# A tile of zeros set by VectorE for TensorE's dummy work at the start of a decoder layer, 17 matmuls in place of 13 transposes

## The chip, the cores and the metric

The kernel runs on one core of one Trainium2 chip. The metric is the time on the device in microseconds (us), the median of several runs. TensorE has two clock levels in what follows, 1.2 and 2.4 GHz.

## The reference

The reference is one hybrid decoder layer over 512 tokens and 1024 channels, all in float32. What is computed first matters here: a projection of the tokens with `w_in`.

```python
proj = h @ w_in[l]                      # (512 x 1024) @ (1024 x 4376)
q, k_c, v_c, k_s, v_s, k_w, v_w, nsa_gl, u, v, merge_gl = jnp.split(proj, splits, axis=-1)
...
o_nsa = native_sparse_attention(q, ...)            # 8 heads, 3 branches
o_sgu = spatial_gating(u, v, ...)
merged = g_nsa * (o_nsa @ w_branch_nsa[l]) + g_sgu * (o_sgu @ w_branch_sgu[l])
mix = merged @ w_out[l]
h = layer_norm(DEEPNORM_ALPHA * h + mix, ln1_g[l], ln1_b[l])
ffn = (jax.nn.silu(h @ w_ffn_gate[l]) * (h @ w_ffn_up[l])) @ w_ffn_down[l]
h = layer_norm(DEEPNORM_ALPHA * h + ffn, ln2_g[l], ln2_b[l])
```

## The kernel before

Each engine has its own instruction list, written out by hand, and the lists meet in semaphores. Every float32 product is made of three matmuls: ScalarE casts an operand to a high part of type float32r (`wh`, `xh`), VectorE subtracts it to get a low part (`wl`, `xl`), and TensorE adds high by high, high by low and low by high into one PSUM bank (`mm3`, line 1639).

The start is what the change touches. SyncE (SP) issues one after the other, for k from 0 to 7, the load of a slice of the transposed x (128 partitions by 512, into `x_sb` in the tile `arena`, line 444) and the load of the slice of `w_in` that goes with it (into `stage`, line 445). ScalarE waits for each and casts it (`hi`, line 688). VectorE takes the low parts in the same order (`lo`, line 1065). Its first instruction of all is the low part of the first x slice, so it waits for ScalarE.

TensorE computes the q projection from these slices: for each k, four blocks of 128 tokens (m) by 512 columns, three matmuls each. For k = 0 and 1 the order is by part, with a wait before each part, so that TensorE begins when the high parts alone are there (`first_part`, line 1661); from k = 2 on it is `mm3`. The next projections (`tokens`) follow, with two units of weights of 512 KB or more each; a unit's low part is made by `split` (line 1055).

Before the slices are there TensorE does dummy work, so as not to stand idle: `awake(13)` transposes the identity tile `ident` 13 times into PSUM bank 3 (through `transpose`, line 1651). Nothing reads the results; the q projection later starts that bank afresh. `ident` is made by GpSimd (POOL) as its first two instructions: a memset (line 521) and an affine select (line 522), the second of which raises `ident_ready`. TensorE waits for `ident_ready` before the dummies. Every later transpose of the kernel uses `ident` too, the first of them after the projection of u has begun.

The tile lists `first` and `second` share the same memory at different times; a tile put into `first` moves the addresses of those after it in `first`. `ident` is float32, so its dummies are float32 transposes.

Of the kernel before, what the change touches and what calls it, by code (L numbers as in the profile page):

```python
# [16 lines left out]
def build_layer(nc, T):  # L17
# [8 lines left out]
    fp32 = mybir.dt.float32  # L26
    f32r = mybir.dt.float32r
# [7 lines left out]
    P = 128  # L35
# [71 lines left out]
    with ExitStack() as ctx:  # L107
        def sb(name, shape, dt, scope=ctx):
            return scope.enter_context(nc.sbuf_tensor(name, shape, dt))

        def sem(name):
            return ctx.enter_context(nc.semaphore(name))
# [14 lines left out]
        ident = sb("ident", [P, P], fp32)  # L127

        first = ExitStack()  # L130
# [25 lines left out]
        ang = sb("ang", [P, 2, MT, HALF], fp32, first)  # L156
        trig = sb("trig", [P, 2, MT, HALF], fp32, first)
        gates = sb("gates", [P, MT, G, R, 3], fp32, first)
        pe_t = sb("pe_t", [P, 2, 16], fp32, first)
        w2 = sb("w2", [P, 3, DH], fp32, first)  # L160
        w2h = sb("w2h", [P, 3, DH], f32r, first)
# [124 lines left out]
        ps = ctx.enter_context(nc.psum_tensor("ps", [P, 8, 512], fp32))  # L286
# [36 lines left out]
        quarter_hi, quarter_lo = sem("quarter_hi"), sem("quarter_lo")  # L323
        x_arrived = [sem(f"x_arrived{k}") for k in range(KD)]
        q_arrived = [sem(f"q_arrived{k}") for k in range(KD)]
        ident_ready = sem("ident_ready")
        small_arrived = sem("small_arrived")
        xt_hi, xt_lo = sem("xt_hi"), sem("xt_lo")
        rows_done = sem("rows_done")
# [719 lines left out]
        def _(dve):  # L1049
# [14 lines left out]
            def lo(dst, src, h):  # L1064
                return dve.tensor_tensor(dst, src, h.bitcast(fp32), ALU.subtract)  # L1065

            def q_lo(k):
                if k % 4 < 3:
                    dve.wait_ge(quarter_hi, 3 * (k // 4) + k % 4 + 1)
                else:  # L1070
                    dve.wait_ge(w_hi, k // 4 + 1)
                lo(w4(wl, k // 4)[:, k % 4, :], w4(stage, k // 4)[:, k % 4, :], w4(wh, k // 4)[:, k % 4, :]).then_inc(
                    quarter_lo if k % 4 < 3 else w_lo, 1)

            for k in range(KD):
                dve.wait_ge(xt_hi, k + 1)
                lo(xl[:, k, :], x_sb[:, k, :], xh[:, k, :]).then_inc(xt_lo, 1)
                q_lo(k)
# [172 lines left out]
            def lo_cmp(w):  # L1251

                dve.wait_ge(ct_hi, w + 1)
                for (dst, src), (h, _) in zip(pair_parts(pcl, CMP_BANK), pair_parts(pch, CMP_BANK)):
                    last = lo(dst, src, h)
                last.then_inc(ct_lo, 1)
# [241 lines left out]
            first, shared = part_sum[:, 0:1, :], part_sum[:, 1:2, :]  # L1498
# [138 lines left out]
        def _(pe):  # L1637
# [12 lines left out]
            def transpose(out, in_, k=P):  # L1650
                return pe.transpose(out, in_, ident[0:k, 0:k])  # L1651

            def awake(n):

                for _ in range(n):
                    transpose(ps[:, 3, 0:P], ident[:, :])

            pe.wait_ge(ident_ready, 1)
            def first_part(m, k, i):
                tok = slice(P * m, P * m + P)  # L1660
                pe.matmul(ps[:, m, :], (xh, xh, xl)[i][:, k, tok], w4((wh, wl, wh)[i], 0)[:, k, :],  # L1661
                          start=k == 0 and i == 0, stop=False)

            awake(13)
            for k in range(2):
                for i, ready in ((0, quarter_hi), (2, xt_lo), (1, quarter_lo)):
                    if i == 0:
# [121 lines left out]
            for g in range(G):  # L1789
                for pp in range(PAIRS):  # L1790
                    pe.matmul(ps[:, g, :], kz[0][:, g, pp, :], q_t(g)[:, HEAD_AT[pp], :], start=pp == 0, stop=False)
                    last = pe.matmul(ps[:, g, :], kz[1][:, g, pp, :], q_t(g)[:, HEAD_AT[pp], :], start=False,
                                     stop=pp == PAIRS - 1)
# [343 lines left out]
```

## Time and profile before

| | us |
|---|---|
| median of 3 runs | 727.62 |
| lowest and highest | 726.94, 727.78 |
| profiled execution, its own time | 727.74 |
| its span, first to last instruction | 726.0 |
| TensorE busy in the span | 714.3 |
| VectorE, ScalarE, GpSimd busy | 512.5, 332.4, 149.2 |

The profile is one execution. Its own time is 1.74 us more than its span, for what lies around the first and last instruction, and 0.12 us more than the median of the runs. PE is TensorE's matmul side, PEld its weight loads, DVE VectorE, ACT ScalarE, POOL GpSimd. Two things are to be known in reading it. A matmul's recorded time is its whole way through the array, so consecutive matmuls overlap; what one costs in a stream is the distance from one start to the next. And a group's start is that of its first instruction, its length that to the end of its last.

### The profile page before, as it was taken

Reading aid. Unit: us, or ns where it says so; the run is one execution under the profiler, and the core shown is the slowest. Engines: PE = TensorE matmul, PEld = TensorE weight load, DVE = VectorE, ACT = ScalarE, POOL = GpSimd, SP = SyncE. Lnnn points to the kernel's source line nnn. Section 1 sums busy time; section 2 is a strip of 40 time slices with the busy share of each in tenths; the row PEclk is TensorE's granted clock in tenths of the full one; section 3 lists DMA queues with packets and bytes.
Section 4 is the critical chain, followed back from the end, with each engine's and each line's share of the span. In section 5 each row is a group of like instructions: output and inputs, shape, how many; then the busy total and the mean of one; then the engine's idle time right before and its main releaser. Section 6 shows DMA issues by size and latency. Waiting matters only on the chain.

```text
span 726.0 us, 11725 instructions
## 1 busy us (share of the span) xinstructions
PE 714.3 (98%) x4312; PEld 635.2 (87%) x4312; DVE 512.5 (71%) x916; ACT 332.4 (46%) x537; POOL 149.2 (21%) x164
## 2 busy tenths in 40 slices
PE   8999999999999999999999999999999999999996
PEld 7889888888888988888899899999999998888885
DVE  5323298797778885665789588899889885223577
ACT  6313576467777777422525154443444443313500
POOL 2516080523243430000000222222222200000000
PEclk9999999999999999999999999999999999999998
DMA  9425243112101204635631133233323334132202
GB/s 294 167 64 170 58 117 116 59 34 83 39 21 59 59 1 116 232 116 189 181 95 59 59 116 87 87 116 116 94 80 116 116 116 159 74 116 89 84 30 87
DMA packets 54611, 73.82 MB, mean 102 GB/s; under 512 B 4144, under 2 KB 40496, under 8 KB 54448
## 3 DMA queue, kind: packets, MB, share of 16 engines
q1 hardware_dynamic: 54432, 72.32, 31.1%
q0 software_dynamic: 144, 1.05, 0.7%
q8 instruction: 21, 0.34, 0.2%
q14 instruction: 14, 0.11, 0.1%
HBM read 70.21 MB, written 2.10 MB: 100 GB/s over the span
## 4 chain that ended last, share of the span: by engine, by line
PE 89%; DVE 5%; ACT 3%; DMA 1%; issue 1%; POOL 0%; DVEq 0%; SPq 0%; ACTq 0%
PE ps L1639 80%; PE ps L1651 3%; PE ps L1647 2%; PE ps L1648 2%; ACT prob L871 1%; DVE wl L1065 1%; PE ps L1661 1%; DMA stage<-in_w_in 1%; DVE ptl L1065 1%; DVE prob L1286 1%; PE ps L2037 0%; DVE vstat L1137 0%; DMA arena<-in_x_t 0%; DVE prob L1240 0%; DVE wl L1055 0%
## 5 line engine op out<-in xcount | busy, mean ns | idle before, releaser
L1639 PE MATMUL ps<-wh,xh 128*128 128x512 f32 (+1 forms) x366 | 140.2, 383 | 0.1
L1639 PE MATMUL ps<-wh,xl 128*128 128x512 f32 (+1 forms) x366 | 139.4, 381 | 0.0
L1639 PE MATMUL ps<-wl,xh 128*128 128x512 f32 (+1 forms) x366 | 139.3, 381 | 0.0
L1639 PE MATMUL ps<-xh,wh 128*128 128x256 f32 (+1 forms) x416 | 135.1, 325 | 0.0
L1055 DVE TENSOR_TENSOR wl<-stage,wh 128x2048 fp32r<-128x2048 f32 (+1 forms) x28 | 63.8, 2277 | 97.4 <-ACT wh L685 64.4
L1639 PE MATMUL ps<-xh,wl 128*128 128x256 f32 (+1 forms) x416 | 131.8, 317 | 0.0
L1639 PE MATMUL ps<-xl,wh 128*128 128x256 f32 (+1 forms) x416 | 131.7, 317 | 0.0
L1639 PE MATMUL ps<-atl,wh 128*128 128x256 f32 (+1 forms) x280 | 86.0, 307 | 0.0
L1639 PE MATMUL ps<-ath,wh 128*128 128x256 f32 (+1 forms) x280 | 86.0, 307 | 0.0
L1639 PE MATMUL ps<-ath,wl 128*128 128x256 f32 (+1 forms) x280 | 86.0, 307 | 0.0
L1639 PEld LDWEIGHTS ps<-xh,wl 128*128 128x128 f32 x416 | 79.3, 191 | 5.4
L1639 PEld LDWEIGHTS ps<-xh,wh 128*128 128x128 f32 x416 | 79.5, 191 | 3.2
L1639 PEld LDWEIGHTS ps<-xl,wh 128*128 128x128 f32 x416 | 79.5, 191 | 3.1
L1639 PEld LDWEIGHTS ps<-wh,xl 128*128 128x128 f32 x366 | 68.7, 188 | 13.3
L1639 PEld LDWEIGHTS ps<-wh,xh 128*128 128x128 f32 x366 | 68.7, 188 | 13.1 <-issue 0.5
L1639 PEld LDWEIGHTS ps<-wl,xh 128*128 128x128 f32 x366 | 68.7, 188 | 12.8
L1065 DVE TENSOR_TENSOR wl<-stage,wh 128x512 fp32r<-128x512 f32 (+1 forms) x72 | 62.3, 877 | 6.9 <-ACT wh L688 3.4
L685 ACT CAST wh<-stage 128x2048 fp32r<-128x2048 f32 x15 | 28.6, 1908 | 76.8 <-PE ps L1639 76.8
L688 ACT CAST wh<-mix 128x1024 fp32r<-128x1024 f32 x36 | 37.6, 1045 | 52.8 <-PE ps L1639 24.0
L630 POOL TENSOR_SCALAR prob<-prob,rinv 128x128 f32<-128x128 f32 (+3 forms) x32 | 41.9, 1310 | 88.8 <-DVE rinv L1237 88.8
L1065 DVE TENSOR_TENSOR wl<-mix,wh 128x1024 fp32r<-128x1024 f32 x36 | 51.5, 1432 | 8.0 <-ACT wh L688 8.0
L1639 PEld LDWEIGHTS ps<-atl,wh 128*128 128x128 f32 x280 | 53.5, 191 | 2.5
(301 smaller groups left out, 1356.0 us busy)
## 6 DMA issues: line engine op xcount, KB each, us to landing
stage<-in_w_in SPq DMA_DIRECT2D x28, 512.0 KB, 4.7
stage<-in_w_ffn_gate SPq DMA_DIRECT2D x22, 512.0 KB, 4.8
stage<-in_w_ffn_up SPq DMA_DIRECT2D x22, 512.0 KB, 4.5
stage<-in_w_ffn_down SPq DMA_DIRECT2D x22, 512.0 KB, 3.8
stage<-in_w_out SPq DMA_DIRECT2D x8, 512.0 KB, 4.6
arena<-in_x_t SPq DMA_DIRECT2D x8, 256.0 KB, 5.3
stage<-in_w_in SPq DMA_DIRECT2D x8, 256.0 KB, 5.5
stage<-in_w_branch_nsa SPq DMA_DIRECT2D x4, 512.0 KB, 7.3
```

The source lines that it names most:

```text
L630: pool.tensor_scalar(prob[:, a % 2, 1, 0:n], prob[:, a % 2, 1, 0:n], rinv[:, a % 2, 1:2], None, ALU.mult).then_inc(p_ok[1], 1)
L685: act.copy(wh[:, slot, :], stage[slot][:, :]).then_inc(w_hi, 1)
L688: return act.copy(dst, src)
L871: act.activation(p, p, ACT.Exp, bias=nmax[:, a % 2, hh:hh + 1], scale=-1.0, accum_out=rsum[:, a % 2, hh:hh + 1]).then_inc(s_exp, 1)
L1055: dve.tensor_tensor(wl[:, slot, 0:n], stage[slot][:, 0:n], wh[:, slot, 0:n].bitcast(fp32), ALU.subtract).then_inc(w_lo, 1)
L1065: return dve.tensor_tensor(dst, src, h.bitcast(fp32), ALU.subtract)
L1286: dve.tensor_tensor_reduce(out=prob[:, a % 2, hh, 0:n], in0=ps[:, hh, 0:n], in1=mask[:, SEQ - n:SEQ], scale=1.0, scalar=-NEG, op0=ALU.add, ...
L1639: return pe.matmul(out, (sh, sh, sl)[i], (mh, ml, mh)[i], start=start and i == 0, stop=stop and i == 2)
L1647: pe.matmul(out, stationary, mh, start=start, stop=False)
L1648: return pe.matmul(out, stationary, ml, start=False, stop=stop)
L1651: return pe.transpose(out, in_, ident[0:k, 0:k])
L1661: pe.matmul(ps[:, m, :], (xh, xh, xl)[i][:, k, tok], w4((wh, wl, wh)[i], 0)[:, k, :], start=k == 0 and i == 0, stop=False)
```

## The change

A tile `zeros` of 128 by 128, float32r, is added after `gates` in `first`, and a semaphore `zeros_ok`. VectorE sets the tile to zero as its first instruction. TensorE waits for `zeros_ok` in place of `ident_ready`, then does 17 matmuls with `zeros` on both sides in place of 13 transposes of `ident`, into the same bank, and then waits for `ident_ready`. GpSimd's list is unchanged.

```diff
+        zeros = sb("zeros", [P, P], f32r, first)
...
-        ident_ready = sem("ident_ready")
+        ident_ready, zeros_ok = sem("ident_ready"), sem("zeros_ok")
...
+            dve.memset(zeros[:, :].bitcast(fp32), 0.0).then_inc(zeros_ok, 1)
             for k in range(KD):
                 dve.wait_ge(xt_hi, k + 1)
                 lo(xl[:, k, :], x_sb[:, k, :], xh[:, k, :]).then_inc(xt_lo, 1)
...
             def awake(n):
 
                 for _ in range(n):
-                    transpose(ps[:, 3, 0:P], ident[:, :])
-
-            pe.wait_ge(ident_ready, 1)
+                    pe.matmul(ps[:, 3, 0:P], zeros[:, :], zeros[:, :], start=True, stop=True)
+
+            pe.wait_ge(zeros_ok, 1)
...
-            awake(13)
+            awake(17)
+            pe.wait_ge(ident_ready, 1)
```

## Rows read from the trace of the kernel before

**Rows 1.** Page: busy time of each engine, share of the span, instructions; the granted clock

```profile
PE 714.3 (98%) x4312; PEld 635.2 (87%) x4312; DVE 512.5 (71%) x916; ACT 332.4 (46%) x537; POOL 149.2 (21%) x164
...
PEclk9999999999999999999999999999999999999998
```

**Rows 2.** Waits of TensorE, whole span: line, whom it waited for, us, times, longest

```profile
PE ps L1651 <- POOL ident L522: 1.6, 1, 1.6
PE ps L1647 <- DVE ptl L1065: 1.4, 5, 0.3
PE ps L1651 <- POOL prob L630: 0.6, 1, 0.6
PE ps L1661 <- ACT wh L688: 0.3, 1, 0.3
PE ps L1639 <- DVE hidl L1065: 0.3, 1, 0.3
```

**Rows 3.** Timeline of TensorE, 0 to 20 us: start, length, instruction [idle before]

```profile
1.59 3.04 PE L1651 MATMUL ps<-ident 128*128 128x128 f32 x13 [1.59 <-POOL ident L522]
4.93 2.05 PE L1661 MATMUL ps<-wh,xh 128*128 128x512 f32 x4 [0.31 <-ACT wh L688]
6.77 1.45 PE L1661 MATMUL ps<-wh,xl 128*128 128x512 f32 x4
8.06 1.09 PE L1661 MATMUL ps<-wl,xh 128*128 128x512 f32 x4
8.98 1.09 PE L1661 MATMUL ps<-wh,xh 128*128 128x512 f32 x4
...
11.72 0.39 PE L1639 MATMUL ps<-wh,xh 128*128 128x512 f32 x1
11.95 0.39 PE L1639 MATMUL ps<-wl,xh 128*128 128x512 f32 x1
```

**Rows 4.** Timeline of TensorE's weight loads and matmuls in narrow windows around 5.9 and 7.4 us

```profile
5.92 0.33 PEld L1661 LDWEIGHTS ps<-wh,xh 128*128 128x128 f32 x1
6.35 0.33 PEld L1661 LDWEIGHTS ps<-wh,xl 128*128 128x128 f32 x1
6.35 0.63 PE L1661 MATMUL ps<-wh,xh 128*128 128x512 f32 x1
7.20 0.56 PE L1661 MATMUL ps<-wh,xl 128*128 128x512 f32 x1
7.60 0.19 PEld L1661 LDWEIGHTS ps<-wh,xl 128*128 128x128 f32 x1
7.60 0.39 PE L1661 MATMUL ps<-wh,xl 128*128 128x512 f32 x1
```

**Rows 5.** Windows of the start and the end: busy time of each engine, then PEclk

```profile
0.00:7.50 7.50, 5.61 (x19) 4.75 (x20) 2.02 (x4) 3.84 (x6) 3.90 (x20) 1.00 0.70 229
...
720.00:726.00 6.00, 0.00 (x0) 0.00 (x0) 3.50 (x12) 0.20 (x1) 0.00 (x0) 0.58 0.23 87
```

**Rows 6.** Timelines of GpSimd, SP, ScalarE and VectorE, 0 to 20 us

```profile
0.80 0.20 POOL L521 MEMSET ident<- 128x128 f32 x1 [0.29 <-POOLq L2120]
1.25 0.28 POOL L522 TENSOR_SCALAR_AFFINE_SELECT ident<-ident 128x128 f32<-128x128 f32 x1 [0.25 <-POOL ident L521]
...
0.80 0.39 SPq L444 DMA_DIRECT2D arena<-in_x_t  x1
...
0.80 1.28 ACT L688 ACT_TABLE_LOAD   x1 [0.80 <-PEq L2120]
3.56 0.62 ACT L688 CAST xh<-arena 128x512 fp32r<-128x512 f32 x1 [1.48 <-DMA arena<-in_x_t]
4.17 0.62 ACT L688 CAST wh<-stage 128x512 fp32r<-128x512 f32 x1
...
4.21 0.69 DVE L1065 TENSOR_TENSOR xl<-arena,xh 128x512 fp32r<-128x512 f32 x1 [4.21 <-ACT xh L688]
```

**Rows 7.** VectorE around a small operation (timeline near the end) and a group of 128x128

```profile
720.06 0.15 DVE L1362 TENSOR_SCALAR nrm<-mv 128x1 f32<-128x1 f32 x1
...
L1240 DVE TENSOR_SCALAR prob<-prob,rinv 128x128 f32<-128x128 f32 x8 | 2.3, 287 | 0.3
```

**Rows 8.** Timeline of TensorE: float32r matmuls of 128 by 128, then float32 transposes

```profile
150.13 0.28 PE L1648 MATMUL ps<-atl,ath 128*128 128x128 f32 x1
150.25 0.27 PE L1647 MATMUL ps<-ath 128*128 128x128 f32 x1
150.36 0.27 PE L1648 MATMUL ps<-atl,ath 128*128 128x128 f32 x1
...
86.66 1.03 PE L1651 MATMUL ps<-ident,arena 128*128 128x128 f32 x8
```

**Rows 9.** Low parts and the work after the start: timelines of VectorE and TensorE

```profile
7.42 0.69 DVE L1065 TENSOR_TENSOR wl<-stage,wh 128x512 fp32r<-128x512 f32 x1
...
8.72 0.69 DVE L1065 TENSOR_TENSOR wl<-stage,wh 128x512 fp32r<-128x512 f32 x1
...
23.03 2.32 DVE L1055 TENSOR_TENSOR wl<-stage,wh 128x2048 fp32r<-128x2048 f32 x1 [6.45 <-ACT wh L679]
...
28.04 0.39 PE L1639 MATMUL ps<-wh,xh 128*128 128x512 f32 x1
```

## The prediction

> **What bounds the kernel now.** I read the busy times first. TensorE is busy 98% of the span, and no other engine over 71% [rows 1]. The waits come next: over the whole span TensorE's matmuls waited for others in nine places, 4.2 us in total, and the longest is the one at the very start, 1.6 us for GpSimd's identity [rows 2]. So almost everything TensorE does is on the path, and what it saves early comes out at the end unless one of the few waits takes it back. What the change can touch lies before the first real matmul and in the clock at which the first real ones run.
>
> The timeline of the start is the view that decides [rows 3]. The 13 dummies run from 1.59 to 4.63 us. TensorE then idles for 0.31 us until ScalarE has the first weights, and the first real matmul begins at 4.93. The first twelve real matmuls (k = 0) take from 4.93 to 8.98, 4.05 us; the next twelve take from 8.98 to 11.72, 2.74 us, the same work. The reader is to see in the narrow windows that this is the clock [rows 4]: from the weight load at 5.92 to the matmul at 7.20 there are three steps of 0.427 us, which for 512 columns is 1.2 GHz, and a weight load takes 0.33 us; from 7.60 on it takes 0.19, and k = 1 has a step of 2.74 / 12 = 0.228 [rows 3], near what 512 columns take at 2.4 GHz. The matmul that starts at 7.20 takes 0.40 to the next, so the rise falls within it, at about 7.57 us. The clock column does not show this: it has 1.00 for 0 to 7.5 us, though it does show the fall in the idle tail, 0.58 [rows 5]. For the start, the distances between starts are the evidence.
>
> The start at 1.2 GHz costs 4.05 - 2.74 = 1.31 us of real work. That is all the change can win there. A microsecond of real matmuls at the low level costs 1 - 0.228 / 0.427 = 0.47 us.
>
> **The change part by part.** *VectorE's memset.* GpSimd, SP and ScalarE all begin at 0.80 us [rows 6], and I take VectorE to do the same. No VectorE memset is in the trace. The nearest rows are 0.15 us for a one-column operation and 0.287 us for 128x128 [rows 7], and GpSimd's memset of the same tile, 0.20 us [rows 6]. I take 0.20, the same operation. It lies beside nothing: VectorE has no other work until 4.21 us [rows 6], and behind it is queued only the first low part, over 3 us later. So its cost on VectorE's path is nothing. TensorE began 0.06 us after the end of the identity (1.25 + 0.28, then 1.59), so it now begins at 0.80 + 0.20 + 0.06 = 1.06, with 1.01 to 1.15 as ends. The dummies lead by 0.53 us.
>
> *Seventeen matmuls for thirteen transposes.* Before, starts were (3.04 - 0.42) / 12 = 0.218 us apart at the low clock, if the last one took 0.42 as the narrowest end. At the high clock a float32r matmul of this shape starts 0.11 after the one before it, and a transpose (1.03 - 0.27) / 7 = 0.109 [rows 8]. The two kinds cost the same, so I take 0.218 for the new ones: 17 x 0.218 = 3.71, free at 4.77 us. The real work can't start before 4.90, since ScalarE ends the first weights at 4.17 + 0.62 = 4.79 [rows 6]. So the four extra ones cost nothing; what hides them is the wait for ScalarE, with 0.13 us to spare. The other end is the low-clock weight load of float32r, 0.33 us [rows 4]: that is a rival below. If the clock rises during the dummies, they end earlier and a gap opens again, without cost by itself.
>
> *The second wait.* `ident_ready` was raised at 1.53 us [rows 6], long before the dummies end, so the moved wait costs nothing. Its cover is the dummies themselves. No DMA moves, and SP's and GpSimd's lists are unchanged. The tiles behind `zeros` move by 512 bytes per partition; no row prices that, and I take nothing, between a hundredth of a per cent either way, as an estimate from the spread of 0.84 us between the runs.
>
> *The rise of the clock.* This is the only term that isn't nothing. Before the rise TensorE did 3.04 us of dummies, idled 0.31, and did 2.64 us of real matmuls. Now the dummies begin 0.53 us earlier, and the gap of 0.31 us closes. The lower end is no move at all, the upper end a rise before 4.93, worth all of the 1.31. Nearest to the rows is a move by what the change adds in front: 0.53 + 0.31 = 0.84 us, worth 0.84 x 0.47 = 0.39 us. The lead alone gives 0.25.
>
> *Does it come through?* With all 1.31 won, k = 1 would start at 7.67 and needs weights cast by then and the low part for its last four matmuls at 9.49; that one ends at 7.42 + 0.69 = 8.11. For k = 2 it ends at 8.72 + 0.69 = 9.41, needed at 10.4. The next projection starts at 28.04, and its low part is ready at 23.03 + 2.32 = 25.35 [rows 9]: 2.7 us of slack against 1.31. After that no wait of TensorE for a load is in the list [rows 2]. So what is late next is nothing, and the gain passes whole.
>
> *The sum*, against the profiled execution: 727.74 - 0.39 = 727.35. The median of the runs is 0.12 below that execution, so 727.2 us.
>
> **The rivals.** *A, the clock is up before the real work.* Matmuls may bring the clock up where transposes didn't. For it: 3.04 us of transposes and 2.64 us of matmuls stood before the rise, and the rise came inside the matmuls. Against it: 0.31 us of idling in between explains as much, and one trace has one rise. It gives 727.62 - 1.31 = 726.3 us. The Trainium skill has a rule for this ("TensorE: Matmul & The Clock Gate", Part 4: PE-mode transpose): transposes do not bring the engine to its full clock, since they aren't counted as work in the same way. By that rule the sum would be this rival's, 726.3, rather than 727.2; that the rise came only after real matmuls agrees with it [rows 3, 4] but doesn't prove it. Chance 0.28.
>
> *B, nothing moves.* The moment of the rise may vary by more from run to run than a lead of half a microsecond moves it; three runs differ by 0.84 us, which is much of 1.31. Then the time is 727.6. Chance 0.17.
>
> *D, the dummies overrun.* If each costs the 0.33 us of a low-clock float32r weight load [rows 4], 17 of them end at 1.06 + 5.61 = 6.67. The real work starts 1.74 late, but with the clock up almost at once: k = 0 would end near 9.4 and not 8.98, so 0.4 to 0.5 us slower, 728.1. Against it: at the high clock these loads (0.19 against 0.14 for transposes) leave the distance at 0.11 [rows 8]. Chance 0.06.
>
> **How the numbers follow.** The forecast, the rise moved by 0.84 us, has 0.40 and gives 727.2. About 0.2% of the time, 1.46 us, is what a measurement of this kernel can tell from no change. Rival A's 1.31 is just under it, so with the spread of runs some 0.11 of its 0.28 passes it: faster 0.12 with a little from the forecast's own tail. Rival C's 1.43 is just under too: slower 0.05. The rest, 0.83, is within 0.2%. The range goes from A less half the runs' spread, 726.3 - 0.4 = 725.9, to B and D with the same, 728.1; C is left out, and a tail of A.
>
> **What would show it.** Right: VectorE's memset at 0.80 for about 0.2 us; the first dummy near 1.06; 17 of them 0.21 to 0.22 apart; first real matmul still at 4.9; the 0.19 us weight loads begin near 6.7 and not 7.6; k = 1 starts near 8.6, and the next projection near 27.6. A shows as k = 1 at 7.7 and dummies that turn faster before they end. B shows as the rise at 7.5 or scattered over executions. C shows as low-clock matmuls after 8. D shows as a first real matmul after 5. The prediction is wrong if the first real matmul isn't held by ScalarE, or if a gain at 12 us isn't there any more at the last matmul.

## The result and the profile after

The changed kernel takes 728.53 us (median of 21 runs, 727.64 to 729.65), the kernel before 727.41 (21 runs beside them, 726.23 to 728.48). The ratio is 1.0016, with a 95% interval of 1.0010 to 1.0022: slower by 1.1 us, beyond the forecast range and on the other side of the forecast. It stays within the 0.2% that the prediction named.

The timelines of the changed kernel's start, of TensorE and of VectorE, answer to [rows 3] and [rows 6].

```profile
1.12 3.89 PE L1658 MATMUL ps<-zeros 128*128 128x128 f32 x17 [1.12 <-DVE zeros L1076]
4.93 2.04 PE L1663 MATMUL ps<-wh,xh 128*128 128x512 f32 x4
6.77 1.63 PE L1663 MATMUL ps<-wh,xl 128*128 128x512 f32 x4
8.24 1.08 PE L1663 MATMUL ps<-wl,xh 128*128 128x512 f32 x4
9.16 1.09 PE L1663 MATMUL ps<-wh,xh 128*128 128x512 f32 x4
...
11.91 0.39 PE L1641 MATMUL ps<-wh,xh 128*128 128x512 f32 x1
...
0.90 0.17 DVE L1076 MEMSET zeros<- 128x128 f32 x1 [0.90 <-PEq L2123]
```

Everything in front of the real work went as planned. VectorE's memset takes 0.17 us, the dummies begin 0.47 us earlier than before, they are (3.89 - 0.42) / 16 = 0.217 us apart, the gap is closed, and the first real matmul starts at 4.93 as before. Only the clock did not follow. The weight loads below, from narrow windows of the timeline, answer to [rows 4]: the low-clock length of 0.33 us still stands at 7.63, and 0.19 comes at 8.01. The rise falls near 7.96 us, not at the 6.7 I had forecast and not even at the 7.57 of before.

```profile
7.63 0.33 PEld L1663 LDWEIGHTS ps<-wh,xl 128*128 128x128 f32 x1
...
8.01 0.19 PEld L1663 LDWEIGHTS ps<-wl,xh 128*128 128x128 f32 x1
```

These two executions differ by 0.19 us at 11.9 us (11.91 against 11.72), and by 0.3 us in their spans (726.3 against 726.0). The medians differ by 1.1. So one profile of each doesn't hold the answer. A guess that the experiments then bear out is that the moment of the rise varies between executions, and that the change moved where it tends to lie. The experiments use many runs for the ratio, and their profiles for the spread.

### The profile page after: what moved, and what is told of

It is laid out like the page before. It is cut to its first block, busy times and chain, and to the rows that moved or that the text cites. A ratio compares the mean times of both kernels' runs of the same rounds, so it can differ in the third digit from the quotient of the medians.

```text
span 726.3 us, 11734 instructions
## 1 busy us (share of the span) xinstructions
PE 715.3 (98%) x4316; PEld 636.4 (88%) x4316; DVE 512.8 (71%) x917; ACT 332.5 (46%) x537; POOL 149.2 (21%) x164
## 4 chain that ended last, share of the span: by engine, by line
PE 90%; DVE 5%; ACT 2%; DMA 1%; issue 1%; POOL 0%; DVEq 0%; SPq 0%; ACTq 0%
PE ps L1641 80%; PE ps L1653 3%; PE ps L1649 2%; PE ps L1650 2%; ACT prob L872 1%; DVE wl L1066 1%; PE ps L1663 1%; DMA stage<-in_w_in 1%; DVE ptl L1066 1%; DVE prob L1288 1%; PE ps L1658 1%; PE ps L2040 0%; DVE vstat L1139 0%; DVE prob L1242 0%; DVE wl L1056 0%
## 5 line engine op out<-in xcount | busy, mean ns | idle before, releaser
L1641 PEld LDWEIGHTS ps<-ath,wh 128*128 128x128 f32 x280 | 53.5, 191 | 2.5
```

What stands on the lines that cost most here:

```text
L1641: return pe.matmul(out, (sh, sh, sl)[i], (mh, ml, mh)[i], start=start and i == 0, stop=stop and i == 2)
```

## The experiments

The letters stand for explanations. Theory K, formed after the result: what helps the clock up depends on the form of the dummy, and float32r matmuls of 128 columns are worth less than the transposes were. Rival Z is rival C of the prediction: it is the data, since zeros switch nothing. Rival L: the time went elsewhere, into moved tiles, a semaphore or other code. All ratios are to the kernel before, run beside each kernel.

**e1, everything but the dummies.**

```diff
-            pe.wait_ge(zeros_ok, 1)
+            pe.wait_ge(ident_ready, 1)
...
-                    pe.matmul(ps[:, 3, 0:P], zeros[:, :], zeros[:, :], start=True, stop=True)
+                    transpose(ps[:, 3, 0:P], ident[:, :])
...
-            awake(17)
-            pe.wait_ge(ident_ready, 1)
+            awake(13)
+            pe.wait_ge(zeros_ok, 1)
```

> The tile, VectorE's memset and the semaphore stay, but TensorE does the 13 transposes of the identity as before. Theory Z (zeros give the clock less than the identity's transposes did, so the rise comes later): as before, ratio 0.9995 to 1.0005. Rival L (the time went elsewhere: moved tiles, one more semaphore, other code): as the changed kernel, ratio 1.0010 to 1.0022. Rival K (the kind of dummy decides, matmul against transpose): as before.

Measured: 727.34 us, ratio 0.9997 (0.9988 to 1.0006). Rival L is out: tile, memset and semaphore cost nothing that shows. The timeline of TensorE in its profiled execution shows the other half of the matter.

```profile
1.59 3.04 PE L1653 MATMUL ps<-ident 128*128 128x128 f32 x13 [1.59 <-POOL ident L523]
4.99 1.42 PE L1663 MATMUL ps<-wh,xh 128*128 128x512 f32 x4 [0.36 <-ACT wh L689]
6.25 1.08 PE L1663 MATMUL ps<-wh,xl 128*128 128x512 f32 x4
```

The same 13 transposes at the same time as before, and yet the first four real matmuls take 1.42 us and not 2.05, and the next four 1.08: the clock was up after some of the first four. Before, it came up after six of them. TensorE's instructions up to there are the same, but for one more wait on a semaphore that had long been raised, and the rises lie about two microseconds apart.

**e2, ones for zeros.**

```diff
-            dve.memset(zeros[:, :].bitcast(fp32), 0.0).then_inc(zeros_ok, 1)
+            dve.memset(zeros[:, :].bitcast(fp32), 1.0).then_inc(zeros_ok, 1)
```

> The changed kernel with ones in the tile in place of zeros, nothing else. Theory Z: the rise comes earlier than in the kernel before, first real matmuls at the high clock or soon after; ratio 0.9982 to 0.9997. Rival K (float32r matmuls of this shape count for less than transposes): no different from the changed kernel, ratio 1.0010 to 1.0022. Rival L: the same as the changed kernel.

Measured: 728.39 us, 1.0015 (1.0006 to 1.0024). The time is that of the changed kernel. This speaks against Z, but ones are one value throughout as well.

**e5, the identity as data, the form of the change.**

```diff
-            dve.memset(zeros[:, :].bitcast(fp32), 0.0).then_inc(zeros_ok, 1)
+            dve.wait_ge(ident_ready, 1)
+            dve.tensor_copy(zeros[:, :], ident[:, :]).then_inc(zeros_ok, 1)
...
-            awake(17)
+            awake(13)
```

> The changed kernel, but VectorE copies the identity into the tile when it is ready, and 13 matmuls of 128 columns are done on it: the kind of the change with the data of before, beginning near 2.0 us. Theory K (float32r matmuls of 128 columns bring the clock up later than transposes do, whatever the data): ratio 1.0006 to 1.0022. Rival Z (what counts is the data, a tile with one value throughout gives nothing): as before, ratio 0.9992 to 1.0006.

Its dummies in the timeline of TensorE:

```profile
1.85 3.03 PE L1659 MATMUL ps<-zeros 128*128 128x128 f32 x13 [1.85 <-DVE zeros L1077]
```

Measured: 728.98 us, 1.0022 (1.0013 to 1.0031). The old data in the new form is as slow as the change, or slower.

**e6, zeros as data, the form of before.** The 13 dummies are `transpose(ps[:, 3, 0:P], zeros[:, :].bitcast(fp32))`; the identity is only what is streamed against them.

```diff
-                    pe.matmul(ps[:, 3, 0:P], zeros[:, :], zeros[:, :], start=True, stop=True)
+                    transpose(ps[:, 3, 0:P], zeros[:, :].bitcast(fp32))
...
-            awake(17)
             pe.wait_ge(ident_ready, 1)
+            awake(13)
```

> The changed kernel, but the dummies are 13 transposes of the tile of zeros by the identity, begun when the identity is ready: the kind of before with the data of the change. Theory K: as before, ratio 0.9992 to 1.0006. Rival Z: as the changed kernel, ratio 1.0006 to 1.0022.

Its dummies in the timeline of TensorE:

```profile
1.68 3.01 PE L1653 MATMUL ps<-ident,zeros 128*128 128x128 f32 x13 [1.68 <-POOL ident L523]
```

Measured: 727.31 us, 0.9998 (0.9989 to 1.0006), the time of before. With e5 this settles data against form: the two kernels swap them, with 13 dummies each over almost the same stretch, and the time goes with the form. A kernel e3, with 17 transposes of zeros against zeros, was planned for the same question and has no time.

**e4 and e11, no dummies at all; e10, the changed kernel once more.** e4 and e11 are the same kernel.

```diff
-            awake(13)
```

> The kernel before without any dummy work. Theory Z, if zeros give nothing at all: as the changed kernel, ratio 1.0010 to 1.0022, with the rise at 8 us or later. If zeros give something: slower than the changed kernel, 1.002 or more. Rival L: the dummies of before are worth an unknown amount; if nothing, ratio 1.0. Rival K: as Z.

> The changed kernel once more, beside e11. Theory P (its dummies are as none at all): ratio as e11 within 0.0004. Theory N (they put the rise off, against no dummies): ratio 1.0012 to 1.0022 and above e11 by 0.0005 or more.

> The kernel without dummies once more, beside e10. Theory P: 1.0009 to 1.0020, as e10. Theory N: 1.0004 to 1.0012, under e10.

Measured: e4 728.02 us, 1.0009 (1.0000 to 1.0018). e11 728.02 us, 1.0012 (1.0003 to 1.0021). e10 728.08 us, 1.0014 (1.0005 to 1.0023). Side by side e10 and e11 are 0.0002 apart. Theory P, that the 17 matmuls are as no dummies at all, allowed up to 0.0004. After e4 alone I had thought that they might even put the rise off (theory N), which asked for 0.0005 or more between the two. So no use of the 17 matmuls shows in the time. That they are worth exactly nothing isn't shown: all four measurements with float32r matmuls of 128 columns (changed, e2, e5, e10: 1.0014 to 1.0022) lie above both without dummies (1.0009 and 1.0012). A part of that may come from elsewhere: both profiles without dummies gained some 0.5 us at 160 us, where nothing of the dummies is left (see below).

The kernel without dummies, e4, starts so:

```profile
5.07 2.04 PE L1661 MATMUL ps<-wh,xh 128*128 128x512 f32 x4 [5.07 <-ACT wh L688]
...
10.33 1.28 PE L1661 MATMUL ps<-wh,xh 128*128 128x512 f32 x4
```

The timeline of e10's profiled execution shows a late rise with the dummies done without a gap:

```profile
1.12 3.89 PE L1658 MATMUL ps<-zeros 128*128 128x128 f32 x17 [1.12 <-DVE zeros L1076]
4.88 2.04 PE L1663 MATMUL ps<-wh,xh 128*128 128x512 f32 x4
6.72 1.91 PE L1663 MATMUL ps<-wh,xl 128*128 128x512 f32 x4
8.43 1.91 PE L1663 MATMUL ps<-wl,xh 128*128 128x512 f32 x4
10.13 1.17 PE L1663 MATMUL ps<-wh,xh 128*128 128x512 f32 x4
```

All twelve matmuls of k = 0 run at 1.2 GHz. TensorE had worked without a stop for 9 us when the clock rose. This is the slowest of e10's eleven runs.

**e7, e9 and e12, wide dummies.** The same zeros, read four times over as 512 columns: nine in e7, eight in e9, and seven in e12 that begin only when the identity is ready.

```diff
-                    pe.matmul(ps[:, 3, 0:P], zeros[:, :], zeros[:, :], start=True, stop=True)
+                    pe.matmul(ps[:, 3, :], zeros[:, :], zeros[:, :].rearrange("p (a n) -> p a n", a=1).broadcast_to([P, 4, P]), start=True, stop=True)
...
-            awake(17)
+            awake(9)
```

> The changed kernel with 9 matmuls of 512 columns of zeros (the tile read four times) in place of 17 of 128: 9 x 0.427 = 3.84 us from 1.12 to 4.96 at the low clock. Theory K: the form of the real work brings the clock up where the narrow one didn't, the first real matmuls run at 2.4 GHz or soon do, ratio 0.9980 to 0.9997, k = 1 starts at 7.7 to 8.6. Rival Z: as the changed kernel, ratio 1.0006 to 1.0022, k = 1 starts after 8.9.

> Eight dummies of 512 columns in place of the nine of e7_wide, which held the first real matmul until 5.13 us. They end near 4.6, so the first real one is at 4.93 again. Theory K: up to 0.2 us better than e7_wide, ratio 0.9978 to 0.9995. If the ninth was needed for the clock: worse than e7_wide, ratio up to 1.0005.

> Seven dummies of 512 columns of zeros, begun only when the identity is ready, from 1.6 to 4.6 us: the stretch of the kernel before, with the wide form. If the form decides: better than before, ratio 0.9980 to 0.9996, near e9. If the earlier beginning decides: as before, 0.9994 to 1.0006.

Measured: e7 726.25 us, 0.9986 (0.9977 to 0.9995). e9 726.23 us, 0.9990 (0.9981 to 0.9999). e12 727.09 us, 0.9993 (0.9984 to 1.0002). So the intent of the change holds once the dummies have the form of the real work. What the early beginning gives isn't settled: e12 has the stretch of before and isn't clear of no change, e9 begins earlier and is, but their intervals overlap. The timeline of TensorE in e7:

```profile
1.12 4.19 PE L1658 MATMUL ps<-zeros 128*128 128x512 f32 x9 [1.12 <-DVE zeros L1076]
5.13 1.13 PE L1663 MATMUL ps<-wh,xh 128*128 128x512 f32 x4
6.09 1.09 PE L1663 MATMUL ps<-wh,xl 128*128 128x512 f32 x4
```

The ninth dummy holds the first real matmul until 5.13, 0.2 us late, and the real ones run at 2.4 GHz nearly from the first. e9 doesn't have that delay (its first real one is at 4.82), and its time is the same: what eight save in front can't be told from the noise.

**e8, the same zeros read as float32**, still 128 columns; eight matmuls, which the trace shows as 16 records.

```diff
-                    pe.matmul(ps[:, 3, 0:P], zeros[:, :], zeros[:, :], start=True, stop=True)
+                    pe.matmul(ps[:, 3, 0:P], zeros[:, :].bitcast(fp32), zeros[:, :].bitcast(fp32), start=True, stop=True)
...
-            awake(17)
+            awake(8)
```

> The changed kernel with 8 matmuls of the same zeros read as float32, 128 columns, which pass the array several times each; 8 x 0.43 = 3.4 us if each costs four passes of 128 columns. Theory K: better than the changed kernel, ratio 0.9980 to 1.0003; how good is open. Rival Z: as the changed kernel, ratio 1.0006 to 1.0022.

Measured: 727.22 us, 0.9998 (0.9989 to 1.0006). The early timeline of e8:

```profile
1.12 3.73 PE L1658 MATMUL ps<-zeros 128*128 128x128 f32 x16 [1.12 <-DVE zeros L1076]
4.95 1.17 PE L1663 MATMUL ps<-wh,xh 128*128 128x512 f32 x4
```

Sixteen records in 3.73 us stand as close as those of the change, and the first real matmuls are fast in this execution, the fastest of the eleven. So it isn't the number of columns alone: read as float32, tiles of the same size do about what the transposes did, and read as float32r they do nothing that shows. The float32 dummies began 0.47 us earlier than the transposes, and over all runs nothing of that shows.

## Where the time lies in all executions

For each profiled execution I take the first real matmul, the start of k = 2 (24 real matmuls on), and subtract 24 x 0.228 = 5.47 us, what they take at 2.4 GHz. What is left is what the low clock cost. The last column is a second witness, which the views of the profile don't show: each trace holds a record of the granted clock, and its first entry, at full clock, begins at this time. All columns but the first two are in us.

| kernel | dummies | first real | k = 2 | cost of the low clock | clock record begins |
|---|---|---|---|---|---|
| before | 13 transposes | 4.93 | 11.72 | 1.32 | 7.55 |
| e1 | 13 transposes | 4.99 | 10.80 | 0.34 | 5.52 |
| e6 | 13 transposes of zeros | 4.96 | 11.22 | 0.79 | 6.52 |
| changed | 17 narrow float32r | 4.93 | 11.91 | 1.51 | 7.94 |
| e10 | 17 narrow float32r | 4.88 | 12.98 | 2.63 | 10.29 |
| e2 | 17 narrow, ones | 4.97 | 12.45 | 2.01 | 9.11 |
| e5 | 13 narrow, identity | 4.92 | 12.02 | 1.63 | 8.21 |
| e4 | none | 5.07 | 13.26 | 2.72 | 10.74 |
| e11 | none | 4.85 | 12.26 | 1.94 | 8.82 |
| e7 | 9 wide | 5.13 | 10.66 | 0.06 | 5.17 |
| e9 | 8 wide | 4.82 | 11.31 | 1.02 | 6.79 |
| e12 | 7 wide, late | 5.08 | 11.80 | 1.25 | 7.55 |
| e8 | 8 float32 | 4.95 | 10.49 | 0.07 | 4.66 |

Does it come through to the end? From k = 2 on, the changed kernel's landmarks lie 0.18 to 0.2 us behind those of before, without change, up to about 155 us. There is one more place where executions differ: a load of weights at 160 us. The chain of waits of before, of the changed kernel and of e10, one after the other:

```profile
158.90 1.15 DVE wl L1065
160.07 0.37 SPq L432
160.48 6.05 DMA stage<-in_w_in
166.55 0.63 ACT wh L882
```

```profile
160.68 6.16 DMA stage<-in_w_in
166.86 0.63 ACT wh L883
```

```profile
160.17 1.15 DVE wl L1066
161.33 0.37 SPq L433
161.75 6.83 DMA stage<-in_w_in
168.59 0.63 ACT wh L883
```

VectorE frees the buffer, SP issues the load, ScalarE waits for it, and TensorE is held through ScalarE. The load took 6.05, 6.16 and 6.83 us; in the executions of e4, e11 and e12 the chain went elsewhere and these gained about 0.5 us on before at this place (from 1.57 us behind to 1.02 in e4). e10 lost 0.77 there (160.17 against 158.90 before the load, 168.59 against 166.55 after it). No edit touches this place, and it adds half to three quarters of a microsecond of spread either way. e7's execution, with next to no cost of the low clock, is still 0.95 us over the median of its runs; 0.5 us of that it lost here. After it the distances stay within about 0.15 us to the last matmul.

## Why the prediction was wrong

**The bound and the cost in front: right.** TensorE's first microseconds do pass to the end. The memset was 0.17 us against 0.20, the start 1.12 against 1.06 (VectorE's first instruction stands at 0.90, not 0.80), the distance 0.217 against 0.218, the first real matmul 4.93, and the moved wait cost nothing. Moved tiles: nothing (e1).

**The rise of the clock: this step failed.** I took the new dummies to help the rise as the old ones did, because they cost the same: 0.11 us apart at the high clock for both kinds [rows 8]. Equal cost told nothing here of what the two do for the clock. The step that failed is the term "a move by what the change adds in front: 0.84 us, worth 0.39". In its place the changed kernel lost what the 13 transposes gave: 1.1 us in the result, and side by side with no dummies at all its ratio is the same within the noise (1.0014 against 1.0012). The clock came up at 7.94 and 10.29 us in its two profiled executions, where I had 6.7. I had nearly this price in hand, as rival C's 1.43, and gave it 0.09.

**Rival C had the side and nearly the size, by a wrong mechanism.** It said zeros. Ones (1.0015) and the identity (1.0022) in the same form are as slow, and transposes of zeros (0.9998) as fast as before.

**Rival A was the wrong way round.** It had matmuls help and transposes not; in the form of the change the matmuls didn't, and the transposes had helped. The rule of the Trainium skill that I cited ("TensorE: Matmul & The Clock Gate", Part 4: PE-mode transpose) says that transposes don't bring the clock up. These runs don't bear it out for float32: without the 13 transposes the kernel takes 1.0009 and 1.0012 of the time, 0.7 to 0.9 us more (the lower of the two intervals begins at 1.0000). The traces say the same: with transposes the clock record begins 0.53 to 2.62 us after the first real matmul (e1, e6, before), without dummies 3.97 and 5.67 us after it (e11, e4). For other types no run here speaks.

**The size of the stake was read from one execution.** I used 1.31 us as what could be won at most. It is 0.34, 0.79 and 1.32 in three executions with transposes. The remark in rival B, that the moment of the rise may vary by more than the lead, was right, but it lies on top of a shift that can be measured; it doesn't cancel it. The changed kernel's own two executions, of one and the same program, have rises 2.35 us apart.

**No wait for a load later: wrong in form.** The list of TensorE's own waits [rows 2] doesn't show the load at 160 us, since ScalarE stands between. It took nothing from the argument, but a part of the spread between runs that I had put down to the clock comes from there.

What stays open is why float32r matmuls of 128 columns don't help while float32 ones at the same distance do, whether they are worth exactly nothing, and how much of e9's gain is the earlier beginning. None of these was tried further.

## What to carry to other kernels

The form of dummy work for the clock has to be tried, and the form of the real work is the first to try: it has the lowest ratios here. Dummies of the same length, distance and data but another form can be worth nothing that shows, and equal cost is no evidence. The test of a dummy is the kernel with none, in many runs, since the rise moves by microseconds between executions of one kernel. Here eight or nine matmuls of 512 columns on a tile that VectorE sets first give 726.2 us, a ratio of 0.9986 to 0.9990, 0.7 to 1.0 us less than before and about 2 us less than the change.

## What the runs showed of the hardware

The moment at which TensorE's clock rises is not fixed by the instruction list: in two executions of the changed kernel it came at 7.94 and 10.29 us, in two without dummies at 8.82 and 10.74. Seventeen float32r matmuls of 128 columns, 0.217 us apart for 3.89 us, gave nothing that shows over no dummies (1.0014 against 1.0012), and after them, in e10, TensorE ran the twelve real matmuls of k = 0 at 1.2 GHz, up to 10.1 us. Thirteen float32 transposes as far apart were worth 0.7 to 0.9 us (e4 and e11).

The clock column of the views shows nothing of all this. In e10, where every matmul up to 10.1 us is at the low level by its distances, a window has (busy time of each engine, then the granted clock, the DMA share and GB/s)

```profile
0.00:8.00 8.00, 6.88 (x25) 6.18 (x25) 2.40 (x5) 4.04 (x6) 3.91 (x20) 1.00 0.75 241
```

